# Attention decays of a gated linear recurrence: exponentials of summed logs, or running products in 32x32 tiles

## The reference, cut to what is computed

```python
bcum = jnp.cumsum(gb, axis=2)                              # gb = log f
rel = bcum[:, :, :, None, :] - bcum[:, :, None, :, :]
decay = jnp.exp(jnp.where(tri, rel, -jnp.inf))
att = jnp.einsum('bhtd,bhsd,bhtsd->bhts', qb, kb, decay)   # k = 1 - f
o = jnp.einsum('bhts,bhsv->bhtv', att, vb) + jnp.einsum('bhtd,bhdv->bhtv', qb * jnp.exp(bcum), S)
S = S * jnp.exp(btot[:, :, 0])[..., None] + jnp.einsum('bhsd,bhsv->bhdv', kb * jnp.exp(btot - bcum), vb)
```

## Time and profile before

| | us |
|---|---|
| median of 3 runs | 1582.16 (1579.61 to 1586.15) |
| profiled execution, span | 1578.4 |
| TensorE busy | 1433.8 (91%) |
| VectorE busy | 543.9 (34%) |
| ScalarE busy | 311.3 (20%) |
| GpSimd busy | 122.4 (8%) |

### The profile page before, as it was taken

The page is one execution under the profiler, slowest core; times in us unless marked ns, Lnnn a source line. Parts: engine busy times, 40 slices in busy tenths (PEclk is TensorE's granted clock), DMA queues, the critical chain, the costliest instruction groups (busy, mean ns, idle before and its releaser), DMA issues.

```text
span 1578.4 us, 46499 instructions
## 1 busy us (share of the span) xinstructions
PE 1433.8 (91%) x20360; PEld 1082.9 (69%) x20361; DVE 543.9 (34%) x1139; ACT 311.3 (20%) x525; POOL 122.4 (8%) x191
## 2 busy tenths in 40 slices
PE   5999999977888999999992899999999999999995
PEld 3698687667777766666461678768768767677672
DVE  4893822747877231211337111101101101011056
ACT  3204023522222610000120111111111111111112
POOL 0060423000000000000002000000000000000020
PEclk9899999888999999999995899999999999999997
DMA  7478623341220011140119891791793999999994
GB/s 306 149 230 318 95 68 96 138 161 62 81 93 15 14 68 53 67 191 22 54 47 379 320 395 31 271 403 30 272 402 126 393 348 395 345 403 342 382 362 176
DMA packets 88135, 319.73 MB, mean 203 GB/s; under 512 B 11632, under 2 KB 11888, under 8 KB 87824
## 3 DMA queue, kind: packets, MB, share of 16 engines
q1 hardware_dynamic: 72288, 268.49, 44.6%
q0 software_dynamic: 13104, 41.00, 8.7%
q10 hardware_dynamic: 2688, 9.44, 2.1%
HBM read 283.73 MB, written 33.06 MB: 201 GB/s over the span
## 4 chain that ended last, share of the span: by engine, by line
PE 74%; DMA 10%; DVE 7%; SPq 4%; ACT 3%; issue 2%; POOL 1%; DVEq 0%; POOLq 0%; ACTq 0%
PE ps L2025 20%; PE ps L1607 10%; PE ps L2012 9%; PE ps L1595 9%; DMA expert_w<-in_w_down 6%; PE ps L1924 4%; PE ps L1960 4%; PE ps L1869 4%; SPq L512 4%; PE ps L1699 2%; DMA expert_w<-in_w_up 2%; PE ps L1782 1%; PE ps L1793 1%; PE ps L1989 1%; DMA weight_ring<-in_stream 1%
## 5 line engine op out<-in xcount | busy, mean ns | idle before, releaser
L2025 PEld LDWEIGHTS ps<-x_block_t,expert_w 128*64 128x64 f32 x14336 | 429.2, 139 | 43.8 <-issue 37.5
L2025 PE MATMUL ps<-x_block_t,expert_w 128*64 128x64 f32 x14336 | 434.1, 223 | 22.3 <-DMA expert_w<-in_w_up 12.3
L2012 PE MATMUL ps<-expert_w,act_t 128*64 128x512 f32 x896 | 209.8, 599 | 3.9 <-DMA expert_w<-in_w_down 3.6
L1607 PE MATMUL ps<-h_t,weight_ring 128*128 128x320 f32 x640 | 176.7, 432 | 0.0
L1525 DVE TENSOR_TENSOR act_t<-silu_tmp,ps 128x64 f32<-128x64 f32 x208 | 46.0, 221 | 365.5 <-ACT silu_tmp L892 365.5
L1607 PEld LDWEIGHTS ps<-h_t,weight_ring 128*128 128x128 f32 x640 | 120.7, 190 | 52.6 <-issue 5.7
L1595 PE MATMUL ps<-h_t,weight_ring 128*128 128x320 f32 x512 | 148.9, 454 | 2.8 <-ACT h_t L673 2.8
L2012 PEld LDWEIGHTS ps<-expert_w,act_t 128*64 128x64 f32 x896 | 59.4, 137 | 108.4 <-issue 103.7
L1595 PEld LDWEIGHTS ps<-h_t,weight_ring 128*128 128x128 f32 x512 | 101.7, 200 | 46.2 <-issue 9.1
L892 ACT ACTIVATE silu_tmp<-ps 128x64 f32<-128x64 f32 x224 | 50.0, 223 | 419.5 <-PE ps L2025 417.8
L1869 PE MATMUL ps<-node_x 128*128 128x128 f32 x560 | 75.4, 294 | 27.9 <-DVE node_x L1278 14.2
(11 more groups left out here) (345 smaller groups left out, 1366.3 us busy)
## 6 DMA issues: line engine op xcount, KB each, us to landing
expert_w<-in_w_gate SPq DMA_DIRECT2D x128, 512.0 KB, 11.0
expert_w<-in_w_up SPq DMA_DIRECT2D x128, 512.0 KB, 12.0
expert_w<-in_w_down SPq DMA_DIRECT2D x128, 512.0 KB, 15.4
weight_ring<-in_stream SPq DMA_DIRECT2D x98, 512.0 KB, 4.8
x_sorted<-zero POOLq DMA_DIRECT2D x18, 512.0 KB, 14.3
x_block<-x_sorted ACTq DMA_DIRECT2D x30, 256.0 KB, 6.1
y_sorted<-y_block POOLq DMA_DIRECT2D x52, 128.0 KB, 5.5
y_sorted<-zero POOLq DMA_DIRECT2D x10, 512.0 KB, 25.4
```

The costliest lines, as they stand in the source:

```text
L1607: last = mm(pair(job)[:, a, :], w[:, k, :], h_t[:, k, a * HALF:(a + 1) * HALF], start=(k == 0), stop=(k == KD - 1))
L2012: last = mm(ps[MB * half:MB * half + MB, 4, :], act_t[:, f, :], w_slot[3 * f + 2][:, 4 * half:4 * half + 4, :].rearrange("p k c -> p (k c) ...
L2025: last = mm(ps[cols, 2 * w + f % 2, 0:MB], w_slot[3 * f + w][:, k, cols], x_blk_t[:, k, :], start=(k == 0), stop=(k == KD - 1))
```

## The change

Decays are now products of the gates themselves, without logs. `kd` (keys, forwards and backwards) and `qd` (queries) are four arrays that hold the decay to the end of their token's node. From one level to the next `lengthen` multiplies, in place, the half that lies farther away by the whole decay of the other half, and `lengthen_decay` doubles the gates' own products. At the five small levels (node sizes 2 to 32) ScalarE joins keys and queries of both directions into `k_both` and `q_both` (`join`), so that one product serves both directions. Products are 32 keys by 32 queries (level 6: 64 by 64), each in its own quarter of the array's columns; they are collected in `att_d`, or copied straight to their place in `att`. The states come behind the levels, as the longest products are the keys that they need. The order of the weight stream, of the jobs and of all engines is laid out anew; `g_t`, `g_hg`, `sig_glu` lie elsewhere; masks shrink from 14x128 to 5x32 columns, constants from 1696 to 448; the loads of `hg_state` wait for level 3's first products.

```diff
-T_Q = (32, 33, 42, 53)
-T_ADA2 = (34, 38, 45, 49, 54)
+T_ADA2 = (36, 41, 46, 50, 55, 60, 65, 70)
+T_GLU = (40, 45)
+T_G = (54, 59, 64, 69)
...
+        k_sum = at("k_sum", ys0, [P, HEADS, TOK])
+        k_both = [at("k_both0", pool0 + 40960, [P, HEADS, TOK]), at("k_both1", pool0 + 61440, [P, HEADS, TOK])]
+        q_both = [at("q_both0", pool0 + 51200, [P, HEADS, TOK]), at("q_both1", pool0 + 71680, [P, HEADS, TOK])]
...
-            pool.wait_ge(y_s5_ready, 1)
+            pool.wait_ge(for_dve, att_job("N31") + 1)
             pool.dma_start(st[:, 0, 0, :, :], hg_state[0, :, :, :].rearrange("h d v -> d h v")).then_inc(hg0_in, 16)
...
-            act.dma_start(cst[:, 384:1664], const[:, 384:1664]).then_inc(reset_in, 16)
...
+            def join(level, pieces):
+
+                half = 1 << level
+                for p in pieces:
+                    src, to = ((kd[0], k_both), (kd[1], k_both), (qd[0], q_both), (qd[1], q_both))[p]
+                    side = (0, 1, 1, 0)[p]
+                    act.wait_ge(piece_ready[p], level + 1)
+                    if level >= 2 and p == 0:
+                        act.wait_ge(for_dve, att_job(f"N{level - 2}1") + 1)
+                    nc.scalar.activation(sides(to[level % 2], half)[side], sides(src, half)[side], ACT.Copy)\
+                        .then_inc(both_ready, 1)
...
+            act.wait_ge(s5_out, 16)
+            join(0, (0, 1))
             take_q(2)
+            take_q(3)
+            join(0, (2, 3))
+            take_ada(0)
             act.wait_ge(g_loaded, 16 * 4)
             take_glu(0)
+            join(1, range(4))
             take_glu(1)
-            exp_keys(0)
+            take_ada(1)
+            join(2, range(4))
...
+            def lengthen(level, pieces):
+
+                half = 1 << level
+                n = HEADS * TOK // (2 * half)
+                for p in pieces:
+                    array, f_all, side = ((kd[0], ff, 0), (kd[1], fb, 1), (qd[0], ff, 1), (qd[1], fb, 0))[p]
+                    if level < SMALL_LEVELS:
+                        dve.wait_ge(both_ready, 4 * level + p + 1)
+                    dve.wait_ge(piece_ready[p], level + 1)
+                    part = sides(array, half)[side]
+                    other = sides(f_all, half)[1 - side][:, :, half - 1:half].broadcast_to((P, n, half))
+                    vec.tensor_tensor(part, part, other, ALU.mult).then_inc(piece_ready[p], 1)
+
+            def lengthen_decay(level):
+                half = 1 << level
+                for p in range(4):
+                    dve.wait_ge(piece_ready[p], level + 2)
+                for f_all in (ff, fb):
+                    left, right = (x[:, :, half - 1:half] for x in sides(f_all, half))
+                    note(vec.tensor_tensor(right, right, left, ALU.mult))
+                settle()
...
+            def take_small(level):
+                dve.wait_ge(mask_ready, 1)
+                for a, (c0, c1) in enumerate(TILE_CHUNKS):
+                    job = att_job(f"N{level}{a}")
+                    n = (c1 - c0) * HEADS
+                    dve.wait_ge(for_dve, job + 1)
+                    took(vec.copy_predicated(att_d[:, c0:c1, :, :].rearrange("p c h t -> p (c h) t"),
+                                             bc(mask[:, level, :], 1, n), compact(job, c1 - c0)), job)
...
-            start_logs(0)
-            start_logs(1)
-            sum_logs(0)
-            sum_logs(1)
...
+            lengthen(2, range(4))
+            lengthen_decay(2)
+            gate_s5(1)
+            vectors2(1)
+            take_small(1)
...
+            take_tiles()
+            lengthen(5, range(4))
+            lengthen_decay(5)
+            vectors2(5)
+            take_halves()
+            lengthen(6, range(4))
+            lengthen_decay(6)
...
+            add_states(0)
+            vectors2(7)
+            add_states(1)
...
+            def tile_products(name, keys, queries):
+
+                for a, (c0, c1) in enumerate(TILE_CHUNKS):
+                    job = att_job(name + str(a))
+                    dve_bank(job)
+                    for n, (c, h) in enumerate(itertools.product(range(c0, c1), range(HEADS))):
+                        for j in range(4):
+                            rows, cols = slice(TILE * j, TILE * j + TILE), slice(c * P + TILE * j, c * P + TILE * j + TILE)
+                            last = mm(bank(job)[rows, TILE * n:TILE * n + TILE], keys[:, h, cols], queries[:, h, cols],
+                                      start=True, stop=True)
...
             project(q_job(1), T_Q + 1)
+            project(q_job(2), T_Q + 2)
+            project(q_job(3), T_Q + 3)
             ada2(0)
+            pe.wait_ge(g_loaded, 16 * 4)
+            glu(0)
+            pe.wait_ge(diag_ready, 1)
+            pe.wait_ge(act_took, q_job(3) + 1)
+            tile_products("D", k_sum, q)
+            select2(0)
+            glu(1)
+            small_level(0)
             ada2(1)
...
+            small_level(4)
+            select2(4)
+            out_gate(1, 0)
+            out_gate(1, 1)
+            pieces_at(5)
+            across("N5", TILE_CHUNKS, TILE)
+            ada2(5)
+            out_gate(2, 0)
+            select2(5)
+            pieces_at(6)
+            across("N6", HALF_CHUNKS, 64)
+            out_gate(2, 1)
+            ada2(6)
+            turn_keys(0)
+            out_gate(3, 0)
+            select2(6)
+            key_values(0)
+            out_gate(3, 1)
+            turn_keys(1)
+            ada2(7)
+            gate(0, (0,))
+            select2(7)
+            key_values(1)
+            gate(0, (1,))
+            pieces_at(LEVELS)
             pe.wait_ge(att_ready, 1)
```

More of the change, by code:

```diff
@@ L19 @@
+import itertools
 import numpy as np
@@ new lines, in take_halves @@
+            def take_halves():
+                for a, (c0, c1) in enumerate(HALF_CHUNKS):
+                    job = att_job(f"N6{a}")
+                    dve.wait_ge(for_dve, job + 1)
+                    src = bank(job)[:, 0:(c1 - c0) * HEADS * 64].rearrange("p (n t) -> p n t", t=64)
+                    for j in range(2):
+                        rows, to = slice(64 * j, 64 * j + 64), 64 * (1 - j)
+                        last = vec.tensor_copy(att[rows, c0:c1, :, to:to + 64].rearrange("p c h t -> p (c h) t"),
+                                               src[rows, :, :])
+                    took(last, job)
@@ L1222, in _ @@
-            vec.nop().then_inc(states_ready, 1)
-            dve.wait_ge(for_act, A["kt"] + 10)
-            vec.tensor_tensor(node_x[1][:, :, :], kf[:, :, :], kb[:, :, :], ALU.add).then_inc(diag_ready, 1)
-            def take_diag():
-                for c in range(CH):
-                    job = V["diag"] + c
-                    dve.wait_ge(for_dve, job + 1)
-                    took(vec.tensor_tensor(att[:, c, :, :], bank(job).rearrange("p (h t) -> p h t", h=HEADS),
-                                           bc(ident, 1, HEADS), ALU.mult), job)
@@ new lines, in small_level, with pieces_at, across @@
+            def small_level(level):
+                pe.wait_ge(both_ready, 4 * level + 4)
+                tile_products(f"N{level}", k_both[level % 2], q_both[level % 2])
+            def pieces_at(level):
+                for p in range(4):
+                    pe.wait_ge(piece_ready[p], level + 1)
+            def across(name, chunks, size):
+                for a, (c0, c1) in enumerate(chunks):
+                    job = att_job(name + str(a))
+                    dve_bank(job)
+                    for n, (c, h) in enumerate(itertools.product(range(c0, c1), range(HEADS))):
+                        for j in range(P // size):
+                            rows = slice(size * j, size * j + size)
+                            own = slice(c * P + size * j, c * P + size * j + size)
+                            other = slice(c * P + size * (j ^ 1), c * P + size * (j ^ 1) + size)
+                            last = mm(bank(job)[rows, size * n:size * n + size], kd[j % 2][:, h, own],
+                                      qd[j % 2][:, h, other], start=True, stop=True)
+                            if a == 0 and n == 0 and j == 0:
+                                first(last)
+                    last.then_inc(for_dve, 1)
@@ new lines, in key_values @@
+            def key_values(d):
+                for n, c in enumerate(KV_CHUNKS[d]):
+                    job = att_job(("KF", "KB")[d] + str(n))
+                    pe.wait_ge(act_took, mid_job("FR"[d], n) + 1)
+                    dve_bank(job)
+                    for h in range(HEADS):
+                        last = mm(bank(job)[:, h * P:(h + 1) * P], kd_t[:, n, h, :], v[:, c, h * P:(h + 1) * P],
+                                  start=True, stop=True)
+                        if h == 0:
+                            first(last)
+                    last.then_inc(for_dve, 1)
```

493 lines of the change are left out of this document (202 added, 291 removed).

## The result

The median went from 1582.6 us (4 runs in this comparison, 1579.6 to 1586.2) to **1487.21 us** (4 runs, 1485.1 to 1491.0): ratio 0.9394, 95% interval 0.9363 to 0.9424. The profiled execution has a span of 1483.2 us at a granted clock of 0.964. The forecast was 1488 (1476 to 1525).

The account below looks back on a forecast made before the run. It took VectorE, always late, with the bank handshake beside it, as the bound. Start 269.4, fixed work 113.4, products 34.8 and waits 6 put the first output product at 423.6, 94 us earlier: 1488 us, range 1476 to 1525.

Parts of the forecast that it names:

- start of the stretch: End of the fourth projection between the S5 outputs, from which TensorE's new program was laid end to end: 269.4 us.
- fixed work: TensorE work that stays (projections, ada groups, GLU and gate products, selections, state products, transposes): 113.4 us.
- products: Seven sets of 160 and 80 level 6 instructions on TensorE, 1200 at 29 ns each: 34.8 us.
- waits, gaps: TensorE's bank handshakes around first small levels and state products, 3 us, plus issue gaps and short clock dips, 3 us.
- lower bound of 6.9: Least ns per small product instruction, 27.3 scaled down to 32 moving columns; would take 26 us off the products.
- row of 27.3 ns: Profile row of the kernel before: 64x32 weights with 128 moving columns, 3.50 us for 128 instructions.
- rival 1: Clock falls as small products use a quarter of the array's columns: 1520 to 1550 us; chance 0.15.
- Rival 2: VectorE becomes the bound through slower multiplications or waits between pieces, a level 16.5 instead of 11.8 us: 1513; chance 0.12.
- upper bound of 2.4: ScalarE's copies of levels 0 and 1, which skip elements, at 2.4 us each instead of 1.25.
- Hidden under 11.8: ScalarE's 6.4 us of work per small level was claimed hidden under TensorE's slot of 11.8 us.
- Rivals 3 and 4: Column tiles don't overlap at low clock, 1677 us, chance 0.06; weight stream or last stage withholds gain, 1508 to 1548, 0.05.
- signs of being wrong: Sets of 8 us or more, TensorE waiting for joined pieces, or in-place multiplications above 1.6 us.

Follow-up runs that it names:

- earlier_gates: Changed kernel reordered as in earlier_select, with the second and third GLU multiplications on VectorE also moved ahead of level 2's and level 3's multiplications: 1487.34 us (0.9364).
- wide_moving: Changed kernel with each small product of the diagonal and five small levels moving all 128 queries instead of 32 past its 32-column weights: 1489.16 us (0.9397).
- before_small: Kernel before the change, with the all-node products of its 14 steps shrunk from 128x128 to 32x32, same instruction count: 1593.12 us (1.003).
- full_size: Changed kernel with the diagonal and five small levels made of 20 full 128x128 products a set instead of 80 of 32x32: 1484.38 us (0.937).
- double_full: Changed kernel with the diagonal and five small levels made of full 128x128 products, each issued twice: 1503.32 us (0.9473).
- vector_load: Changed kernel with each of the four GLU multiplications on VectorE done three times, same result: 1501.0 us (0.9459).
- earlier_select: Changed kernel reordered: VectorE's products of the second ada step ahead of lengthening level 2's decays, ScalarE's level 2 copies ahead of the second sigmoid: 1488.78 us (0.9377).

## Why the prediction was right

The time was right within 1 us and so was its place. Within 1 us is luck: the same kernel, measured again beside `earlier_gates`, had a median of 1496.14. And the sum came out only because its errors cancelled: with the measured 15.1 us of products and all else as forecast it would have been 1468, below the stated range. Its terms against what TensorE's rows show up to 422.8:

| term | predicted | measured |
|---|---|---|
| start of the stretch | 269.4 | 272.9 |
| fixed work | 113.4 | 116.9 (132.0 busy less the products) |
| products | 34.8 | 15.1 (diagonal 1.6, levels 0 to 4 9.0, level 5 1.9, level 6 2.6) |
| waits, gaps | 6 | 17.8 |
| sum | 423.6 | 422.7 |

- **Products, the mis-sized term.** Each of the 160 instructions of a set takes 10 ns, not 29. The rows at hand move 64 and 128 columns, and most of the time goes with the columns: `wide_moving` took 28.6 ns at 128, of which a quarter is 7.1. The lower bound of 6.9 was nearer than the value I took, and the range left it out: its low ends, 1478 and 1476, have no room for the 26 us that this bound takes off. The Trainium skill (TensorEngine Tiling (Array Packing), Instruction Overhead) gives each matmul about 60 cycles, by which that bound fell away. Counted per instruction, as the prediction did, the trace speaks against it: 10 ns are 24 cycles of 2.4 GHz. Counted per fp32 product of two instructions it is 48, not far from the rule, so the unit in which I read it may be part of the error. The row of 27.3 ns, which the prediction found to agree, moved 128 columns and could not test it.
- **Waits, the other one.** The 3 us for gaps and dips were 8.2 us of issue gaps alone, and the 3 us for handshakes were 9.4, of which 4.5 at one place. That place is the order on VectorE: the bank that TensorE wants is released behind level 2's multiplications. The prediction compared lane totals per level (10.5 to 11.5 against 11.8) and didn't ask which instruction of a lane the other waits for.
- **Start and fixed work.** At 206 to 224 us (granted clock 0.76 from 210 on) the products with `m_lhs` took 7.32 us where the next took 5.83, and the projection behind them 10.56 where the next took 8.88, which is nearly all of the 3.5. The change didn't do this: `before_small`, which is the old kernel up to there, has the same 7.29 for the products with `m_lhs` where the profile of before has 5.83. Inside the part a GLU product took 6.04 and half a gate 6.23 instead of 4.57. So rival 1 (the clock falls) came at a few us, not 30, and not by its cause: the sets beside 297 and 306 us ran at clock 1.00, and the low clock stands behind a wait, 4.54 us idle, then 64 instructions at 17 ns each and the GLU product of 6.04.
- **VectorE.** Most operations were costed well: in-place multiplications 1.41 from start to start (1.49 each), masked copies 0.6 and 0.45, level 4's multiplications done at 341 (predicted 340), waits of VectorE for TensorE from level 3 on (3.8, 7.0, 9.5 us). The pair of decays was not: 2.6 in level 1 where 1.6 was the most that was costed, and 1.4 in level 2. Rival 2 (VectorE the bound, 1513) was half true, by its waits between pieces and up to level 2.
- **ScalarE.** Its copies took 1.25 to 1.45, the 1.25 of the sum. Levels 0 and 1, which touch every other float and every other pair, were 0.1 to 0.2 longer, and the upper bound of 2.4 is out. The Trainium skill (SBUF — State Buffer, Specifications) says that two hits in a 16-byte line are enough for full bandwidth. These rows agree with it nearly. "Hidden under 11.8" was wrong: doubled, they passed on three quarters.
- **Weight stream and what lies behind.** Stream waits fell from 7.1 to 0.2 as forecast, and 227 and 833 us stayed. Rivals 3 and 4 are out.
- **The signs.** Of those named for being right, four came: the output product near 423, no stream waits up to 300, the copies' time (nearly), and the stretches behind. Three didn't: sets of 4.4 to 5 us (1.6), clock 1.00 from 290 on (0.94 from 310 to 400), and TensorE busy for over 0.9 of the stretch (0.88). Of the signs of being wrong none came.

## What to carry to other kernels

When engines hand pieces to each other in a loop, compare not lane totals but the place in each lane at which the next engine's resource comes free; doubling one lane's work shows in one run whether it is hidden. A right total proves no term: check each against its own row. Making products smaller can trade array time for gaps of issue, so count the instructions as well as the columns.

## What the hardware showed

- A weight load of 128x32 with its product of 32 moving columns took 10 ns on TensorE at clock 1.00 when four column groups take turns, 160 of them in 1.6 us; at clock 0.50 it took 17 ns (64 in 1.08 us).
- At that rate TensorE stopped for 0.7 to 2.3 us at distances of 127 pairs or multiples of it, and for up to 4.8 us when twice as many instructions were issued. With full-size products, which took more array time in a quarter of the instructions, there was no such gap (`full_size`, `double_full`). The Trainium skill (Runtime: NRT & Kernel Launch, Instruction fetch mechanics) says that instructions are refilled in blocks of 256 and that this is hidden behind the pace at which they are dispatched. The distance agrees nearly. If the gaps are these refills, which no run here tested, they aren't hidden for such short instructions.
- A long idle time of TensorE was followed by work at the lower clock: a GLU product took 6.04 us behind 4.54 us of waiting, 6.76 behind 9.48 (`vector_load`), and 4.57 where the wait was 0.39 (`earlier_select`). So such a wait costs more than its own length. Not every wait does so, and not every fall has one: behind 2.30 us idle at 308 to 310 us the GLU product took 4.58, and from 206 to 224 us TensorE was busy throughout at a mean clock of 0.81.
